# Sparse layers' first four blocks take the residual before its norm; the forget gate moves behind the remainders

## What is computed

```python
for l in range(2):
    h = rmsnorm(x, norm_g[l])      # x * rsqrt(mean(x*x) + eps) * g
    proj = h @ w_in[l]             # queries, keys, values, gates, pool, conv, fox, merge
    ...                            # four branches out of proj, among them
    logf = log_sigmoid(f_logit + f_bias); c = cumsum(logf)   # the forget gate of fox
    x = x + acc @ w_out[l]
return rmsnorm(x, final_norm_g)
```

## Time and profile before

| | |
|---|---|
| median of 3 runs | 2412.28 us (2409.51 to 2415.3) |
| profiled execution | 2415.88 us, its span 2414.2 us |
| TensorE matmuls busy | 2219.8 us, 92% |
| VectorE, ScalarE, GpSimd busy | 1091.6, 1014.9, 826.0 us |
| mean granted TensorE clock | 0.958 of full |
| HBM traffic | 189.43 MB, mean 78 GB/s |

### The profile page before, as it was taken

The page is one execution under the profiler, slowest core; times in us unless marked ns, Lnnn a source line. Parts: engine busy times, 40 slices in busy tenths (PEclk is TensorE's granted clock), DMA queues, the critical chain, the costliest instruction groups (busy, mean ns, idle before and its releaser), DMA issues.

```text
span 2414.2 us, 31738 instructions
## 1 busy us (share of the span) xinstructions
PE 2219.8 (92%) x11292; PEld 1817.1 (75%) x11292; DVE 1091.6 (45%) x1926; ACT 1014.9 (42%) x1911; POOL 826.0 (34%) x364
## 2 busy tenths in 40 slices
PE   5988988799998887999998989999998989999997
PEld 4776766687887776888887777777776777777776
DVE  5698898434535135423215523222354523222364
ACT  5756675724234333323322323444632323444631
POOL 2422222143445212444442333333343433333342
PEclk9999999889999997999997899999999999999998
DMA  3221111132333211333332222222233322222231
GB/s 136 79 62 48 61 53 51 57 101 86 97 97 113 70 38 41 96 96 96 96 97 83 87 79 61 70 71 70 72 95 90 102 76 70 70 71 70 70 96 61
DMA packets 51742, 189.43 MB, mean 78 GB/s; under 512 B 6564, under 2 KB 7204, under 8 KB 51108
## 3 DMA queue, kind: packets, MB, share of 16 engines
q1 hardware_dynamic: 48096, 175.13, 24.4%
q10 hardware_dynamic: 2452, 6.88, 0.8%
q0 software_dynamic: 1072, 5.77, 0.6%
HBM read 185.66 MB, written 2.10 MB: 78 GB/s over the span
## 4 chain that ended last, share of the span: by engine, by line
PE 68%; DVE 15%; issue 6%; ACT 5%; DVEq 4%; POOL 2%; DMA 0%; POOLq 0%; ACTq 0%
PE bank L335 19%; PE bank L337 18%; PE bank L336 18%; PE bank L866 2%; PE bank L909 2%; POOL weight_lo L366 1%; PE bank L892 1%; ACT weight_hi L361 1%; DVE attention_work L1600 1%; ACT wide_region L991 1%; DVE wide_region L1977 1%; PE bank L409 1%; DVE work_region L1624 1%; DVEq L1566 1%; DVE wide_region L1980 1%
## 5 line engine op out<-in xcount | busy, mean ns | idle before, releaser
L366 POOL TENSOR_TENSOR weight_lo<-weight_slots,weight_hi 128x1024 fp32r<-128x1024 f32 x286 | 691.8, 2420 | 1157.7 <-ACT weight_hi L361 1157.7
L361 ACT ACTIVATE weight_hi<-weight_slots 128x1024 fp32r<-128x1024 f32 x286 | 303.0, 1061 | 855.5 <-PE bank L337 783.9
L335 PE MATMUL bank<-h_hi,weight_hi 128*128 128x512 f32 x1248 | 510.3, 409 | 33.8 <-DVE fq_lo L1841 14.5
L336 PE MATMUL bank<-h_lo,weight_hi 128*128 128x512 f32 x1248 | 494.2, 396 | 0.0
L337 PE MATMUL bank<-h_hi,weight_lo 128*128 128x512 f32 x1248 | 494.1, 396 | 0.0
L335 PEld LDWEIGHTS bank<-h_hi,weight_hi 128*128 128x128 f32 x1248 | 239.1, 192 | 91.0 <-issue 19.4
L337 PEld LDWEIGHTS bank<-h_hi,weight_lo 128*128 128x128 f32 x1248 | 238.9, 191 | 52.1
L336 PEld LDWEIGHTS bank<-h_lo,weight_hi 128*128 128x128 f32 x1248 | 239.7, 192 | 44.5
L366 POOL TENSOR_TENSOR head_weight_lo<-weight_slots,head_weight_hi 128x1024 fp32r<-128x1024 f32 x42 | 104.3, 2485 | 293.1 <-ACT head_weight_hi L361 293.1
L335 PE MATMUL bank<-h_hi,head_weight_hi 128*128 128x512 f32 x336 | 139.1, 414 | 5.6 <-DVE h_lo L383 3.1
L336 PE MATMUL bank<-h_lo,head_weight_hi 128*128 128x512 f32 x336 | 132.6, 395 | 0.0
(11 more groups left out here) (439 smaller groups left out, 4307.4 us busy)
## 6 DMA issues: line engine op xcount, KB each, us to landing
weight_slots<-weights SPq DMA_DIRECT2D x328, 512.0 KB, 3.6
wide_region<-cmp_w ACTq DMA_DIRECT2D x2, 2048.0 KB, 8.0
v_region<-ssm_bc POOLq DMA_DIRECT2D x8, 256.0 KB, 4.7
residual<-x_in POOLq DMA_DIRECT2D x1, 2048.0 KB, 9.0
out<-normed SPq DMA_DIRECT2D x4, 512.0 KB, 2.7
residual<-x_in SPq DMA_DIRECT2D x2, 512.0 KB, 5.6
residual<-x_in ACTq DMA_DIRECT2D x2, 512.0 KB, 10.1
v_region<-mem_in POOLq DMA_DIRECT2D x1, 1024.0 KB, 5.1
```

What stands on the lines that cost most here:

```text
L335: pe.matmul(to, w_h[:, k, :], hi[:, k, 0:width], start=(k == 0), stop=False)
L336: pe.matmul(to, w_h[:, k, :], lo[:, k, 0:width], start=False, stop=False)
L361: act.activation(parts[0][s % 2], slot[s], ACT.Copy).then_inc(w_hi[s], 1)
L366: eng.tensor_tensor(parts[1][s % 2], slot[s], parts[0][s % 2].bitcast(F32), ALU.subtract).then_inc(w_lo[s], 1)
```

## The change

1. Blocks 0 to 3 of each layer multiply T = x g, split into scaled_hi (ScalarE, a Copy with the gain as scale) and scaled_lo (VectorE). They go to banks 0 to 3 without reuse. VectorE applies the root where it empties the banks (scaled_out), with TOKENS, the spread root copied to SBUF. ScalarE no longer empties them. H is still made, and used from block 4 on.
2. At seam A T follows residual_add tile by tile, blocks 0 and 1 run together by k with norm 7's sums between, and the spread stands in the middle of block 2. VectorE empties banks 0 and 1 before it splits H, 2 and 3 after. At seam B T is made under the last product of layer 0; norm 8's sums stand in block 0, its spread in block 1; all four banks are emptied after the split.
3. Blocks 1 and 3 have weight parts of their own (in score_parts), so that the parts of blocks 0 to 2 are made before or during the seam. ScalarE's program holds the rounding of block 3 ahead of H's roundings; blocks 4 and 5 follow within or behind them.
4. The remainders fq_lo 1, fk_lo 0, nq, ks, kw and fk_lo 1 stand ahead of the forget gate.
5. On all engines but SyncE the loop over layers is written out; GpSimd keeps its inner loop over quads. The transfer of lvecs moves: layer 0's to the start, layer 1's into layer 0's attention (step 8, behind conv_out).

```diff
-S_H, S_OBR, S_ACC, SL = (KT * i for i in range(4))
+S_T, S_H, S_OBR, S_ACC, SL = (KT * i for i in range(5))
...
+        T_HI, T_LO = rounded("scaled_hi", "wide_region", 0, 8), rounded("scaled_lo", "work_region", 0, 8)
+        W_NEXT = [[W_MAIN[n][0], side, W_MAIN[n][1], side]
+                  for n, side in enumerate(rounded(f"next_weight_{part}", "score_parts", 2 * n, KT, P)
+                                           for n, part in enumerate(("hi", "lo")))]
...
+            def scaled_terms(s, k):
+                w_h, w_l = W_NEXT[0][s], W_NEXT[1][s]
+                pe.matmul(bank[s][:, :], w_h[:, k, :], T_HI[:, k, :], start=(k == 0), stop=False)
+                pe.matmul(bank[s][:, :], w_h[:, k, :], T_LO[:, k, :], start=False, stop=False)
+                mm = pe.matmul(bank[s][:, :], w_l[:, k, :], T_HI[:, k, :], start=False, stop=(k == KT - 1))
+                if k == KT - 1:
+                    mm.then_inc(mm_done[s], 1)
+
+            for L in range(LAYERS):
+                q0 = QL * L + Q_L2
+                for s in range(2):
+                    pe.wait_ge(evac_done[s + 2], q0)
+                if L == 0:
+                    pe.wait_ge(var_ready, 7)
+                    for s in range(2):
+                        pe.wait_ge(w_lo[s], q0 + 1)
+                    for k in range(KT):
+                        pe.wait_ge(lo_ready, S_L2 + S_T + (k + 1))
+                        for s in range(2):
+                            scaled_terms(s, k)
+                        pe.wait_ge(sq_ready, 7 * KT + (k + 1))
+                        mm = norm_terms(pe, k, k == 0, k == KT - 1, TT, SQ)
+                    mm.then_inc(ms_ready, 1)
+                else:
+                    pe.wait_ge(w_lo[0], q0 + 1)
+                    for k in range(KT):
+                        pe.wait_ge(lo_ready, SL * L + S_L2 + S_T + (k + 1))
+                        if k == KT - 2:
+                            norm_sums(pe, L + 7, L + 6)
+                        scaled_terms(0, k)
+                    pe.wait_ge(w_lo[1], q0 + 1)
+                    for k in range(KT):
+                        if k == KT // 2:
+                            norm_spread(pe, L + 7)
+                        scaled_terms(1, k)
+                pe.wait_ge(w_lo[2], q0 + 1)
+                for k in range(KT):
+                    if L == 0 and k == KT // 2:
+                        norm_spread(pe, L + 7)
+                    scaled_terms(2, k)
+                pe.wait_ge(w_lo[3], q0 + 1)
+                for k in range(KT):
+                    scaled_terms(3, k)
+                pe.wait_ge(evac_done[0], q0 + 1)
+                gemm(pe, q0 + 1, 0, H_HI, H_LO, T, SL * L + (S_L2 + S_H), own_bank=True)
...
-                norm_sums(pe, L + 8, L + 7)
+            norm_sums(pe, 9, 8)
...
+            def next_weight_hi(quad, s):
+                act.wait_ge(w_full[s], 16 * quad + 16)
+                if s == 0:
+                    act.wait_ge(mm_done[2], quad)
+                elif s == 2:
+                    act.wait_ge(mm_done[3], quad)
+                elif s == 3:
+                    act.wait_ge(mm_done[1], quad + 1)
+                act.activation(W_NEXT[0][s], slot[s], ACT.Copy).then_inc(w_hi[s], 1)
+
+            def scaled_hi(k):
+                act.activation(T_HI[:, k, :], X[:, k, :], ACT.Copy,
+                               scale=LVEC[:, L_NORM + k:L_NORM + k + 1]).then_inc(hi_ready, 1)
+
             act.wait_ge(ms_ready, 6)
             for blk in range(KT):
                 s, quad = blk % 4, Q_L2 - 2 + blk // 4
                 if blk < KT - 2:
                     ahead(act, quad, s)
+                elif blk == KT - 1:
+                    next_weight_hi(Q_L2, 1)
+                    next_weight_hi(Q_L2, 0)
                 act.wait_ge(evac_done[s], quad + 1)
                 act.activation(SQ[:, blk, :], YF[:, blk, :], ACT.Square).then_inc(sq_ready, 1)
+            next_weight_hi(Q_L2, 2)
             act.wait_ge(ms_ready, 7)
-            squares_of_sum(act, 3)
-
-            with act.Fori(0, LAYERS) as L:
-                q0 = act.snap(QL * L + Q_L2)
-                stages = act.snap(SL * L + S_L2)
-                def layer(ap):
-                    return ap[bass.ds(L, 1)].rearrange("a p n -> (a p) n")
+            act.wait_ge(lvec_in, 16)
+            for k in range(KT):
+                act.wait_ge(x_ready, 2 * KT + (k + 1))
+                scaled_hi(k)
+                act.activation(SQ[:, k, :], X[:, k, :], ACT.Square).then_inc(sq_ready, 1)
...
-                weight_hi(act, q0, 0)
-                weight_hi(act, q0, 1)
-                act.wait_ge(lvec_in, 16 * L + 16)
+                    act.dma_start(dst, src[L]).then_inc(lw_in, 16)
+                act.dma_start(R[:, 24 * T:32 * T], cmp_w1[L]).then_inc(w1_in, 16)
+                next_weight_hi(q0, 3)
                 for k in range(KT):
+                    if L == 0 and k == 2:
+                        weight_hi(act, q0 + 1, 0)
                     round_hi(act, stages + S_H, k, H_HI[:, k, :], H[:, k, :])
+                if L > 0:
+                    weight_hi(act, q0 + 1, 0)
+                weight_hi(act, q0 + 1, 1)
...
-                store(q0, 0, RAW[:, 0, :], 64 ** -0.5)
-                store(q0, 1, RAW[:, 1, :], 64 ** -0.5)
-                store(q0, 2, RAW[:, 2, :])
-                store(q0, 3, KCVC)
...
+                            if L + 1 < LAYERS:
+                                act.dma_start(LVEC[:, :], lvecs[L + 1]).then_inc(lvec_in, 16)
...
+                    elif blk == KT - 1 and L + 1 < LAYERS:
+                        next_weight_hi(q0 + QL, 1)
+                        next_weight_hi(q0 + QL, 0)
                     act.wait_ge(evac_done[s], quad + 1)
                     act.activation(SQ[:, blk, :], X[:, blk, :], ACT.Square).then_inc(sq_ready, 1)
+                    if L + 1 < LAYERS:
+                        if blk == 0:
+                            act.wait_ge(lvec_in, 16 * L + 32)
+                        scaled_hi(blk)
+                if L + 1 < LAYERS:
+                    next_weight_hi(q0 + QL, 2)
...
-            residual_add(dve, 6, YF, vec(V_FF_POST))
-
-            with dve.Fori(0, LAYERS) as L:
-                q0 = dve.snap(QL * L + Q_L2)
-                stages = dve.snap(SL * L + S_L2)
+
+            def scaled_lo(k, stage):
+                dve.wait_ge(hi_ready, stage + (k + 1))
+                dve.scalar_tensor_tensor(T_LO[:, k, :], X[:, k, :], LVEC[:, L_NORM + k:L_NORM + k + 1],
+                                         T_HI[:, k, :].bitcast(F32), ALU.mult, ALU.subtract).then_inc(lo_ready, 1)
+
+            dve.wait_ge(bc_ready, 7)
+            dve.wait_ge(lvec_in, 16)
+            for k in range(KT + 2):
+                if k < KT:
+                    op = dve.scalar_tensor_tensor(YF[:, k, :], YF[:, k, :], column(V_FF_POST + k), bank[7][:, :],
+                                                  ALU.mult, ALU.mult)
+                if k == KT - 1:
+                    op.then_inc(bc_used, 1)
+                if 1 <= k <= KT:
+                    dve.tensor_tensor(X[:, k - 1, :], X[:, k - 1, :], YF[:, k - 1, :], ALU.add).then_inc(x_ready, 1)
+                dve.drain()
+                if k >= 2:
+                    scaled_lo(k - 2, S_L2 + S_T)
+            dve.sem_inc(t_ready, KT)
+
+            for L in range(LAYERS):
+                q0 = QL * L + Q_L2
+                stages = SL * L + S_L2
                 norm_root(dve, L + 7)
-                dve.wait_ge(lvec_in, 16 * L + 16)
+                dve.wait_ge(bc_ready, L + 8)
+                dve.tensor_copy(TOKENS, bank[7][:, :])
+                dve.drain()
+
+                def scaled_out(s):
+                    dve.wait_ge(mm_done[s], q0 + 1)
+                    dst = (RAW[:, 0, :], RAW[:, 1, :], RAW[:, 2, :], KCVC)[s]
+                    dve.scalar_tensor_tensor(dst, bank[s][:, :], 64 ** -0.5 if s < 2 else 1.0, TOKENS,
+                                             ALU.mult, ALU.mult).then_inc(evac_done[s], 1)
+
+                if L == 0:
+                    scaled_out(0)
+                    scaled_out(1)
                 norm_split(dve, L + 7, stages + S_H, H, H_HI, H_LO, X, LVEC[:, L_NORM:L_NORM + KT])
+                for s in range(2 if L == 0 else 0, 4):
+                    scaled_out(s)
+                dve.drain()
...
+                rest_out(1, q0 + 1, 3, FQ_LO[1], FQ_HI[1], 64 ** -0.5)
+                rest_out(2, q0 + 2, 0, FK_LO[0], FK_HI[0])
+                dve.wait_ge(nq_hi, L + 1)
+                for i in range(2):
+                    dve.tensor_tensor(NQ_LO[i], NQ_SUM[:, i, :], NQ_HI[i].bitcast(F32), ALU.subtract)
+                dve.tensor_tensor(KS_LO, KS_SUM, KS_HI.bitcast(F32), ALU.subtract)
+                dve.tensor_tensor(KW_LO, KW_SUM, KW_HI.bitcast(F32), ALU.subtract).then_inc(nq_ready, 1)
+                rest_out(3, q0 + 2, 1, FK_LO[1], FK_HI[1])
...
-                rest_out(1, q0 + 1, 3, FQ_LO[1], FQ_HI[1], 64 ** -0.5)
```

(28 more changed lines are left out.)

30 lines of the change are left out of this document (13 added, 17 removed).

## The result

The changed kernel takes **2376.2 us** (median of 4 executions, 2374.7 to 2377.2); the kernel before takes 2410.9 beside it (4 executions, 2409.1 to 2415.3). The ratio is 0.9853, with a 95% interval of 0.9836 to 0.987: 34.7 us faster. The prediction was 2374.5 us within 2363 to 2390. The sum is right; two of its terms are off by 5 and 4 us in opposite directions, and most of a third came from somewhere else than the prediction put it.

A forecast was written before the change was run, and what follows sets the result against it. TensorE's matmuls were taken as the bound (busy 92%), time being won only where it waits or runs at lower clock; 12.5 + 7.0 + 18.5 = 38.0 us off 2415.9 gave 2377.9, or 2374.5 on the median's scale, range 2363 to 2390.

The forecast's parts named there:

- Part 1: Both sparse layers: with remainders ahead of the forget gate, TensorE no longer waits or drops to half clock; 18.5 us.
- The cover: VectorE's idle time before the pooling, 29 us left a layer, hides the moved gate arithmetic, costed at nothing.
- Part 2: Entry into sparse layer 0: products start on the unnormalised residual times gain as it appears; 12.5 us saved.
- two k at half and six at full: Entry into layer 0: two of eight tiles' products and sums at half clock, six at full; 7.2 + 13.9 us.
- The 6 us for the rise: Entry into layer 0: the clock needs about 6 us of products at half speed before it rises, as before.
- The rival: Entry into layer 0: sums between products keep the clock low, all tiles at half; 25.3 us left, 2387; 15 in 100.
- The row of 434 to 438: Profile window with short idle stretches and clock 0.84, cited as showing that short pauses can lower the clock.
- Part 3: Between layers 0 and 1: squares and split ride in the last blocks; 9.0 us less one clock fall of 2.0: 7.0.
- The prediction's chain: Between layers 0 and 1: step-by-step timing to the end of blocks 4 and 5 at 1901.3, holding no loop-jump idle time.
- Part 4: Loop over layers written out: no gain added beyond the work between layers, and no charge for fresh code.
- Layer 1, 9.25: Second sparse layer's body: shorter by the removed remainder waits of 7.23 us and half-clock loss of 2.05.

The follow-up runs named there:

- gate_only: Kernel before, with only the query and key remainders moved ahead of the forget gate in both sparse layers: 2386.0 us, ratio 0.9896 to before.
- unrolled: Kernel before, with only the loops over the two sparse layers written out on all engines: 2405.0 us, ratio 0.9966 to before.
- gate_unrolled: Kernel before, with the forget gate moved and the loops written out, but no late normalisation: 2386.9 us, ratio 0.9899 to before.
- seams_only: Changed kernel with the forget gate put back ahead of the remainders, loops still written out: 2399.9 us, ratio 0.9946 to before.
- sums_behind: Changed kernel with the eight sets of one-column sums entering layer 0 put behind the products of blocks 0 and 1: 2378.1 us, ratio 0.9859 to before.
- gate_x4: Changed kernel in which VectorE writes the forget gate's last six operations four times with the same values: 2376.1 us, ratio 0.9853 to before.

## Why the prediction was right, and where it was not

**Part 1, the gate, 18.5.** Right in mechanism and size: 9.4 us a layer at the place itself. The cover was put at 29 us; 25.4 are idle ahead of the pooling, and it is 40 by the run that exceeded it. What the prediction did not have is that the time behind also changes: 0.2 us more in layer 0 and 3.5 more in layer 1, by the clock at the entry of the attention. Over pairs of kernels that differ in the gate alone the ratios are 0.0104 (gate_only), 0.0067 (unrolled against gate_unrolled) and 0.0093 (seams_only against changed) apart: 25, 16 and 22 us for the same edit, each known to 4 to 6 us, so that 18.5 fits the last two and falls just short of the first.

**Part 2, seam A, 12.5.** 7.4 measured. The first product came 11.4 us after the feed-forward products (11.0 predicted). The term that failed is "two k at half and six at full", 21.1 us; it measured 25.9, because four slices ran at half clock, and a set of sums at half clock cost 1.7 (4.27 less six products of 0.427) instead of 1.05. A row in hand had that price: 64 of these rows' matmuls, eight sets, took 13.78 at half clock, 1.72 a set. The 6 us for the rise were taken from a stretch of products alone. The rival named the cause, that the sums "stand between the products", and put it too high (all eight at half). Behind the sums all went as written: root 1.9, spread 1.05, two evictions 1.29; one meeting with GpSimd of 2.81 where 2.19 was assumed; block 5's weight 1.14 late, where 2.1 was reckoned.

The rule of the Trainium skill cited there ("TensorE: Matmul & The Clock Gate", A second HAM failure mode) explains a swinging clock by short idle stretches between groups of matmuls. At seam A the opposite happened: TensorE had no idle stretch from 1308.8 to 1325.3 and stayed low, and in sums_behind it had gaps and rose. The rule speaks of idle stretches, so it gives no reason for the rival at seam A; the rival's own reason, the sums between the products, is the one that the runs bear out. At the entry of the attention the rule fits what was seen: falls of the clock behind pauses of 1.36 and 1.56 us, and none in the four layers where they are filled. The row of 434 to 438 that the prediction leans on is no good example of dense work: TensorE is busy for 1.09 of its 4 us.

**Part 3, seam B, 7.0.** 7.2 measured; waits 2.56 and 3.02 (2.5 and 3.3 predicted), one fall of the clock for eight products, 1.9 (2.0), 43.5 us from the last block to the swap (41.5 and the 2.0). But 4.5 of the 7.2 come from the loop written out (46.1 in unrolled and gate_unrolled), and 2.6 from the late normalisation. The prediction's chain left the jump out and so had the sum right; it did not say that most of this term needs nothing of the new arithmetic.

**Part 4, no loop.** Put at nothing. Fresh code costs nothing, that half is right: 488.4 and 483.9 in unrolled. The loop itself is worth 4.5 to 4.9 us at seam B, which sits in part 3's sum; in the medians writing it out is worth 8 us in one pair and nothing in the other.

**Layer 1, 9.25.** 12.95 measured, 3.3 of the surplus by the fall of the clock that layer 1 escaped. This is a term that the prediction lacked; it made up for most of seam A's shortfall. So the closeness of 2374.5 to 2376.2 owes something to two errors of opposite sign, and 1.4 us to a kernel before that ran at 2410.9 instead of 2412.3: the gain was put at 38.0 and measured 34.7 in the medians, 40.2 in the two profiled executions.

## What to carry to other kernels

Cost a stretch of matmuls by what is in it, not by how busy the engine is: one-column products between wide ones kept the clock at half for 15.9 us instead of 5.5, and summing squares on an idle VectorE won 6 us. Before crediting a rewritten seam to its new arithmetic, run the loop written out alone: here it had 4.5 of 7.2 us. And where TensorE pauses for a microsecond or two, fill the pause with products that have to be done anyway; it gives the pause back, and the clock behind it stayed up in the four layers tried.

## What the runs showed of the hardware

One-column products in a row let a risen clock fall: 1.00 until 1328.5 and 0.50 from 1328.7, without an idle stretch (sums_behind). Set between wide products at half clock, they put off its rise from 5.5 to 15.9 us. The same instructions with the same pauses of 1.36 and 1.56 us ran at either clock from layer to layer, up to 3.3 us apart. A loop over layers cost 4.5 and 4.9 us at the seam between its two passes. VectorE's TENSOR_SCALAR (L1976 in gate_x4) took 0.55 us alone and 2.5 to 2.7 beside GpSimd's weight remainders.
